# The start of a two-layer encoder: x turned into six banks, scaled parts taken straight from them, and the norm from sums along rows

## What is computed

```python
h = rmsnorm(x, norm_w)                       # x * rsqrt(mean(x*x) + 1e-6) * norm_w
proj = jnp.einsum('bsd,de->bse', h, w_in)    # 1024 -> 9 sections of 1024
qa, ka, va, ga, qh, ffw, fbw, ih, gh = split_cols(proj, EVEN_SIZES)
oa = differential_attention(qa, ka, va, ...) * silu(ga)      # 8 heads
ob = hgrn2_bidirectional(qh, ffw, fbw, ih, ...) * silu(gh)   # 8 heads
x = x + jnp.einsum('bse,ed->bsd', concatenate([oa, ob]), w_out)
```

## Time and profile before

| | before |
|---|---|
| median of 3 executions | 1157.49 us (1157.34 to 1159.63) |
| the profiled execution | 1158.41 us, of it 1156.6 us span |
| TensorE matmul busy | 1127.6 us, 97% |
| DVE busy | 977.4 us, 85% |
| ACT busy | 677.1 us, 59% |
| mean granted TensorE clock | 0.997 |

### The profile page before, as it was taken

How to read it: one execution, slowest core, us unless ns; L and a number is a source line. 1 busy time by engine, 2 the same in 40 slices (tenths; PEclk the granted TensorE clock), 3 DMA queues, 4 the chain that set the end, 5 groups by cost and what they waited for, 6 DMA issues and landing times. The chain is left out here.

```text
span 1156.6 us, 18631 instructions
## 1 busy us (share of the span) xinstructions
PE 1127.6 (97%) x5750; PEld 913.4 (79%) x5750; DVE 977.4 (85%) x1927; ACT 677.1 (59%) x1324; POOL 0.2 (0%) x4
## 2 busy tenths in 40 slices
PE   6999999999999999999999999999999999999996
PEld 5877778778778778778778877887888888888875
DVE  6879889889889889789789898888888888888886
ACT  6474564564564564564654674366666666666654
POOL 0000000000000000000000000000000000000000
PEclk9999999999999999999999999999999999999999
DMA  7613422522422423323324220554232324323112
GB/s 211 158 56 92 138 64 56 145 65 58 130 73 61 121 73 75 107 73 86 96 73 98 85 73 19 124 137 122 80 91 54 91 66 120 101 59 91 55 38 73
DMA packets 131817, 103.60 MB, mean 90 GB/s; under 512 B 5440, under 2 KB 116416, under 8 KB 131776
## 3 DMA queue, kind: packets, MB, share of 16 engines
q1 hardware_dynamic: 131776, 103.07, 32.7%
HBM read 77.88 MB, written 2.10 MB: 69 GB/s over the span
## 5 line engine op out<-in xcount | busy, mean ns | idle before, releaser
L74 PE MATMUL bank_proj<-hH,w_hi 128*128 128x512 f32 x856 | 343.1, 401 | 1.3 <-issue 1.2
L76 PE MATMUL bank_proj<-hH,w_lo 128*128 128x512 f32 x856 | 334.5, 391 | 0.0
L75 PE MATMUL bank_proj<-hL,w_hi 128*128 128x512 f32 x856 | 334.3, 391 | 0.0
L76 PEld LDWEIGHTS bank_proj<-hH,w_lo 128*128 128x128 f32 x856 | 160.8, 188 | 35.2
L74 PEld LDWEIGHTS bank_proj<-hH,w_hi 128*128 128x128 f32 x856 | 161.5, 189 | 32.8 <-issue 1.9
L75 PEld LDWEIGHTS bank_proj<-hL,w_hi 128*128 128x128 f32 x856 | 161.4, 189 | 30.9 <-issue 0.5
L1943 ACT ACTIVATE probs<-bank_odd_score,small 128x256 f32<-128x256 f32 (+1 forms) x128 | 66.3, 525 | 73.9 <-DVE small L2181 73.9
L1220 DVE TENSOR_TENSOR w_lo<-w_raw,w_hi 128x1024 fp32r<-128x1024 f32 x74 | 89.4, 1217 | 9.3 <-ACT w_hi L710 9.3
L710 ACT ACTIVATE w_hi<-w_raw 128x1024 fp32r<-128x1024 f32 x74 | 78.0, 1055 | 28.9 <-DMA w_raw<-in_w_in_even 28.4
L1950 ACT ACTIVATE probsT<-bank_odd_turn 128x256 fp32r<-128x256 f32 (+1 forms) x128 | 49.0, 434 | 61.8 <-PE bank_odd_turn L1677 61.7
L775 ACT ACTIVATE probs<-bank_score,small 128x512 f32<-128x512 f32 x64 | 43.4, 684 | 60.0 <-DVE small L1058 53.2
(11 more groups left out here) (412 smaller groups left out, 2219.0 us busy)
## 6 DMA issues: line engine op xcount, KB each, us to landing
w_raw<-in_w_in_even SPq DMA_DIRECT2D x72, 512.0 KB, 4.9
w_raw<-in_w_in_odd SPq DMA_DIRECT2D x36, 512.0 KB, 4.4
qs<-parts SPq DMA_DIRECT2D x96, 128.0 KB, 2.3
ks<-parts SPq DMA_DIRECT2D x40, 256.0 KB, 4.4
o_raw<-in_w_out_even SPq DMA_DIRECT2D x15, 512.0 KB, 6.2
o_raw<-in_w_out_odd SPq DMA_DIRECT2D x14, 512.0 KB, 6.7
out<-w_raw SPq DMA_DIRECT2D x8, 256.0 KB, 2.1
mixT<-in_x SPq DMA_DIRECT2D x2, 512.0 KB, 5.4
```

Of the source, the lines that this page charges most:

```text
L74: pe.matmul(out, hi, moving_hi, start=start, stop=False)
L75: pe.matmul(out, hi, moving_lo, start=False, stop=False)
L76: return pe.matmul(out, lo, moving_hi, start=False, stop=stop)
```

## The change

SP issues the first weight (-2) between the two halves of x. TensorE turns the eight tiles into six banks (S[0], S[1], T, O, W, PB[2], and S[0], S[1] again), so only tiles 6 and 7 wait: 6 for the first low part and the copy of tile 0, 7 for the copy of tile 1. ACT and DVE form hH and hL straight out of the banks. The copies to xT come later: tile 0 on ACT, all others on DVE, six of them behind the low part of the second weight. On ACT the first weight's high part comes behind the first tile; on DVE its low part too.

The norm's squares are taken from x by rows: four ACT squares of 128 x 1024 with a sum along the row (their own output goes to scratch), into four columns x_squares. One DVE copy spreads each column over 128, and four transposes on TensorE, behind six eighths of projection -1, put the sums of all rows in every partition of T. The root on ACT stands ahead of the high part of weight 1 and not behind it.

On DVE rope scaling comes ahead of the low part of weight 1; the lambda products and the low part of weight 2 come between the first rotation and the values. On TensorE the turning of the values stands behind five eighths of projection 1 and not behind two.

```diff
--- before.py
+++ after.py
@@ -124,12 +124,14 @@
         self.high, self.low = map(sem, ("high", "low"))
         self.xT, self.w, self.hH, self.hL = xT, w, hH, hL
 
-    def split_high(self, act, k):
-        act.activation(self.hH[:, k], self.xT[:, k], ACT.Copy, scale=self.w[:, k:k + 1]).then_inc(self.high.sem, 1)
-
-    def split_low(self, dve, k):
+    def split_high(self, act, k, of=None):
+        of = self.xT[:, k] if of is None else of
+        act.activation(self.hH[:, k], of, ACT.Copy, scale=self.w[:, k:k + 1]).then_inc(self.high.sem, 1)
+
+    def split_low(self, dve, k, of=None):
+        of = self.xT[:, k] if of is None else of
         dve.wait_ge(self.high.sem, self.high.at(0, k + 1))
-        dve.scalar_tensor_tensor(out=self.hL[:, k], in0=self.xT[:, k], scalar=self.w[:, k:k + 1],
+        dve.scalar_tensor_tensor(out=self.hL[:, k], in0=of, scalar=self.w[:, k:k + 1],
                                  in1=self.hH[:, k].bitcast(F32), op0=ALU.mult,
                                  op1=ALU.subtract).then_inc(self.low.sem, 1)
 
@@ -206,6 +208,7 @@
         row_sum, weight = small[:, 16:24], small[:, 24:32]
         lam_t, lam_e = small[:, 32:33], small[:, 34:36]
         total = small[:, 40:48].rearrange("p (d c) -> p d c", d=2)
+        x_squares = small[:, 48:48 + NC]
         att = attT[:, 0:NC * SEQ].rearrange("p (s t) -> p s t", s=NC)
         att_diag = attT[:, :].rearrange("p (c w) -> p c w", w=SEQ + P)[:, :, 0:P]
         key_sum = attT[:, NC * SEQ:2560]
@@ -220,6 +223,9 @@
         O, W = Bank(nc, ctx, "out", 6, -4), Bank(nc, ctx, "wide", 4, -3)
 
         T = Bank(nc, ctx, "turn", 8, 0)
+
+        XB = [S[0], S[1], T, O, W, PB[2], S[0], S[1]]
+        KEPT = (1, 2, 5, 3, 4, 6, 7)
 
         x_landed = [sem(f"x_landed{i}", unit=DMA) for i in range(2)]
         landed = sem("constants_landed", unit=DMA)
@@ -319,10 +325,11 @@
         def _(sp):
             sp.dma_start(eye[:], eye_d).then_inc(x_landed[0].sem, DMA)
             sp.dma_start(wn[:, 0], norm).then_inc(norm_landed.sem, DMA)
-            for i in range(2):
+            def load_x(i):
                 for a in range(2):
                     part = x[2 * a * P:2 * (a + 1) * P, i * SEQ:(i + 1) * SEQ].rearrange("(t p) d -> p t d", p=P)
                     sp.dma_start(x_tiles[a][:, :, i * SEQ:(i + 1) * SEQ], part).then_inc(x_landed[i].sem, DMA)
+
             def load(h, n):
 
                 if w_low.due(h, n - 3):
@@ -377,7 +384,9 @@
                         sp.dma_start(ks[HD * twice:HD * twice + HD, c, :, :].bitcast(F32),
                                      parts[HD * c:HD * c + HD, :, :].bitcast(F32)).then_inc(k_moved.sem, DMA)
 
+            load_x(0)
             load(0, -2)
+            load_x(1)
             load(0, -1)
             sp.dma_start(rope[:], rope_d).then_inc(rope_landed.sem, DMA)
             load(0, 0)
@@ -428,10 +437,12 @@
             for k in range(KT):
                 if k % 4 == 0:
                     pe.wait_ge(x_landed[k // 4].sem, x_landed[k // 4].at(0, 2 if k else 3))
-                if k >= 2:
-                    pe.wait_ge(x_kept[k % 2].sem, x_kept[k % 2].at(0, k // 2))
+                if k == 6:
+                    pe.wait_ge(raw.low.sem, raw.low.at(0, 1))
+                if k >= 6:
+                    pe.wait_ge(x_kept[k % 2].sem, x_kept[k % 2].at(0, 1))
                 for t in range(NC):
-                    mm = pe.transpose(S[k % 2][:, t * P:(t + 1) * P], x_tiles[t // 2][:, t % 2, k * P:(k + 1) * P],
+                    mm = pe.transpose(XB[k][:, t * P:(t + 1) * P], x_tiles[t // 2][:, t % 2, k * P:(k + 1) * P],
                                       eye[:])
                 mm.then_inc(x_turned.sem, 1)
             pe.wait_ge(ready.sem, ready.at(0, 5))
@@ -577,14 +588,19 @@
                 values(h, 1, vh, att)
 
             proj(0, -2)
-            proj(0, -1, 0, 5)
-            rms.sum(pe, T)
-            proj(0, -1, 5)
+            proj(0, -1, 0, 6)
+            pe.wait_ge(rms.added.sem, rms.added.at(0, 1))
+            pe.wait_ge(x_kept[1].sem, x_kept[1].at(0, 2))
+            for t in range(NC):
+                mm = pe.transpose(T[:, t * P:(t + 1) * P], x_rstd[:, t * P:(t + 1) * P], eye[:])
+            mm.then_inc(rms.summed.sem, 1)
+            proj(0, -1, 6)
+            pe.wait_ge(x_kept[1].sem, x_kept[1].at(0, 3))
             proj(0, 0)
-            proj(0, 1, 0, 2)
+            proj(0, 1, 0, 5)
             pe.wait_ge(PB[2].free.sem, PB[2].free.at(0, 0))
             turn(0, 1, vt)
-            proj(0, 1, 2)
+            proj(0, 1, 5)
 
             def iteration(h, first, last):
 
@@ -692,13 +708,14 @@
         @block.scalar
         def _(act):
             act.preload_act_table_set(EXP_LOG)
-            def keep_x(k):
+            def keep_first_x():
+                act.wait_ge(x_turned.sem, x_turned.at(0, 1))
+                act.wait_ge(raw.low.sem, raw.low.at(0, 1))
+                act.activation(xT[:, 0], XB[0][:], ACT.Copy).then_inc(x_kept[0].sem, 1)
+
+            def high_x(k):
                 act.wait_ge(x_turned.sem, x_turned.at(0, k + 1))
-                act.activation(xT[:, k], S[0][:], ACT.Copy).then_inc(x_kept[0].sem, 1)
-
-            def high_x(k):
-                act.wait_ge(x_kept[k % 2].sem, x_kept[k % 2].at(0, k // 2 + 1))
-                raw.split_high(act, k)
+                raw.split_high(act, k, XB[k][:])
 
             def high(h, n):
 
@@ -849,25 +866,21 @@
                         place.then_inc(bank.free.sem, 1)
 
             act.wait_ge(norm_landed.sem, norm_landed.at(0, 1))
-            keep_x(0)
             high_x(0)
+            high(0, -2)
             high_x(1)
-            keep_x(2)
-            high_x(2)
-            high_x(3)
-            keep_x(4)
-            high(0, -2)
-            high_x(4)
-            high_x(5)
-            keep_x(6)
-            high_x(6)
-            high_x(7)
+            keep_first_x()
+            for k in range(2, KT):
+                high_x(k)
             high(0, -1)
-            for k in range(KT):
-                rms.square(act, k)
+            for t, into in enumerate((decay, soft, turned, probs)):
+                for i in range(2):
+                    act.wait_ge(x_landed[i].sem, x_landed[i].at(0, 2 if i else 3))
+                act.activation(into[:, :, :].rearrange("p a t -> p (a t)"), x_tiles[t // 2][:, t % 2, :], ACT.Square,
+                               accum_out=x_squares[:, t:t + 1]).then_inc(rms.squared.sem, 1)
             high(0, 0)
+            rms.root(act, T)
             high(0, 1)
-            rms.root(act, T)
             act.wait_ge(lam_steps.sem, lam_steps.at(0, 2))
             act.activation(lam_e, lam_e, ACT.Exp).then_inc(lam_steps.sem, 1)
             high(0, 2)
@@ -993,7 +1006,7 @@
 
             def keep_x(k):
                 dve.wait_ge(x_turned.sem, x_turned.at(0, k + 1))
-                dve.tensor_copy(xT[:, k], S[1][:]).then_inc(x_kept[1].sem, 1)
+                dve.tensor_copy(xT[:, k], XB[k][:]).then_inc(x_kept[1].sem, 1)
 
             def scale(h, n, into):
 
@@ -1243,29 +1256,27 @@
                                     chunked(bank[:])).then_inc(bank.free.sem, 1)
 
             dve.wait_ge(norm_landed.sem, norm_landed.at(0, 1))
-            keep_x(1)
-            raw.split_low(dve, 0)
-            raw.split_low(dve, 1)
-            keep_x(3)
-            raw.split_low(dve, 2)
-            keep_x(5)
-            raw.split_low(dve, 3)
+            low_x = lambda k: raw.split_low(dve, k, XB[k][:])
+            low_x(0)
             low(0, -2)
-            raw.split_low(dve, 4)
-            keep_x(7)
-            for k in range(5, KT):
-                raw.split_low(dve, k)
+            low_x(1)
+            keep_x(KEPT[0])
+            for k in range(2, KT):
+                low_x(k)
             low(0, -1)
-            for k in range(1, KT):
-                rms.add(dve, k)
+            for k in KEPT[1:6]:
+                keep_x(k)
+            dve.wait_ge(rms.squared.sem, rms.squared.at(0, NC))
+            dve.tensor_copy(chunked(x_rstd[:]), x_squares.unsqueeze(2).broadcast_to([P, NC, P])).then_inc(rms.added.sem, 1)
+            keep_x(KEPT[6])
             low(0, 0)
+            scale_rope()
             low(0, 1)
+            rotate(-1, 7)
             first_lambda()
-            scale_rope()
-            rotate(-1, 7)
+            low(0, 2)
             scale_vt(0, 0, 0)
             rotate(-1, 8)
-            low(0, 2)
             last_lambda()
             scale(0, 1, keys[:, 0])
 
```

## The result

| | before | after |
|---|---|---|
| median of 12 executions each | 1157.88 us | 1159.76 us |
| lowest to highest | 1156.38 to 1159.63 | 1158.74 to 1162.06 |
| the profiled execution | 1158.41, span 1156.6 | 1159.89, span 1157.6 |

The ratio after to before is 1.002, with a 95% interval of 1.0013 to 1.0027: the change costs 1.9 us. That is the direction of the forecast and less than half of its size (4.65 over its own base, 4.2 over this one). Of the 1.9 us, 0.4 lie outside the span, which runs from the first to the last instruction: time less span is 1.72 to 1.90 in every execution of before whose span is on record, and 2.11 to 2.29 in the twelve of after. No profile shows what this is.

What follows compares the result with a forecast made beforehand. TensorE, busy 97%, was taken as the bound, with two chains meeting at the scores. 2.95 later there plus 1.7 for the clock made 4.65: 1163.1 for the profiled execution, 1162.1 forecast, range 1157.0 to 1164.5.

Steps and rivals of the forecast that it cites:

- x and the first weight: Load queue at the start: x's second half lands at 12.2 to 12.3, the first weight at 9.1.
- The turning of x: TensorE's first transposes: waits for x till 12.3, projection starts at 15.8 instead of 16.12, full clock rate at 16.7.
- the rival with the full rate early: TensorE at full rate when x's second half lands: projection at 14.6, total 1158.8 or 1160.5; chance 0.20.
- Scaled parts out of banks: DVE's eight splits reading banks instead of SBUF: 751 against 743 ns each, so no cost.
- The edits ahead of the root bring 0.35: TensorE's chain up to the norm's root: root at 28.0 instead of 28.34, all earlier edits together gaining 0.35 us.
- The new order behind the root, + 3.3: DVE between root and second rotation: added work less removed waits 3.46, taken as 3.3 us after overlap.
- Sum at the scores, 49.2: Start of the first scores: 46.27 - 0.35 + 3.3 = 49.2, or 2.95 us later than before.
- The clock behind that wait, + 1.7: After TensorE's wait ahead of the scores the granted clock falls, costing 1.7 us (ends 0 and 1.7).
- the first rival: The clock stays up at the scores: same chain, 2.95 later, 1160.4 us; chance 0.18.
- the forecast's own case: Scores 2.95 us later plus a clock fall of 1.7: 1161.0 to 1163.5 us; chance 0.36.
- The faster rival: At the 105.70 wait, DVE's own chain comes earlier and the clock does not fall: - 2.9, 1154.6 us; chance 0.12.

Runs made afterwards that it cites:

- after_again: The changed kernel once more, an unaltered copy: 1160.93 us, ratio 1.0024 to before.
- norm_alone: The kernel before with only the new norm (four row squares, one copy, four transposes): 1156.46 us, ratio 0.9987 to before.
- tail_alone: The kernel before with only the new order of work behind the norm's root, old beginning and old norm kept: 1162.12 us, ratio 1.0037 to before.
- lambda_early: The changed kernel with DVE's two lambda products moved ahead of rope scaling, into the wait for the root: 1159.32 us, ratio 1.0015 to before.
- old_tail: The changed kernel with the order of work behind the norm's root put back as before: 1156.61 us, ratio 0.999 to before.

## Why the prediction was right, and where its size was not

- **x and the first weight.** Right: x's second half was issued at 3.78 and landed 8.4 later, at 12.18 (forecast 12.2 to 12.3), and TensorE had a wait there, 0.92.
- **The turning of x.** The middle value, 15.8 with the lower rate to 16.7, is what three of four executions show (15.25 to 15.85, and the products of 512 columns are down to 0.42 or less from 16.68 to 17.19 on); the profiled one took the course of the rival with the full rate early (13.95, there 14.6), and by the times so, it seems, did ten of 22. Both were forecast, and which one an execution takes is not in the program. The Trainium skill, TensorE: Matmul & The Clock Gate (Part 1: The HAM clock gate), says the same of runs of one program, and these four agree: 46.96 to 49.37.
- **Scaled parts out of banks.** Right. DVE's low part lasts 742 to 746 ns out of any bank in after (up to 749 in after_again), 743 out of SBUF before (746 in norm_alone). The 62 cycles more that the Trainium skill, VectorE: DVE Perf Modes (The TRN2 errata), gives an instruction from PSUM do not show.
- **The edits ahead of the root bring 0.35.** Rope scaling is at 27.65, 27.83 and 28.14 in three executions against 28.49 before, so 0.84, 0.66 and 0.35, and 2.81 in the one with the early full rate. norm_alone, at 27.32 with x 0.4 later, adds that the norm is the part that gains.
- **The new order behind the root, + 3.3.** Right in kind and size: from rope's scaling to the scores 17.78 before, 21.28 in after, 21.11 in after_again, 20.91 in tail_alone: + 3.1 to 3.5. The wait between lambda and weight 2 is 1.22 (forecast 1.3), the wait for the values 1.32 (1.6), the wait at the scores 3.03 (2.6). lambda_early, built to take 1.8 of its terms out, brought the scores 1.86 forward.
- **Sum at the scores, 49.2.** 48.76 to 49.37 in three of four executions.
- **The clock behind that wait, + 1.7: this is the term that failed.** The step said that since 2.44 idle at 105.70 brought the clock down, a longer wait would. In none of four executions of the changed kernel did it, after up to 3.03 idle. In tail_alone and lambda_early, with 2.65 and 2.67 idle, it did, for 1.4 and 1.5. The length of the wait does not order them. The price was about right, the rule not, and I had given it 1.7 where it should have been a case beside the other. Without it the forecast is 1160.4, that is the first rival, against the measured 1159.76 and 1160.93. That 1160.4 lies so near is in part luck: the forecast has one course where the kernel has two (scores 0.69 later in one profile, 2.49 to 3.10 in three), and it has no term for the 0.4 outside the span. The median of the first series lies in its stated range and below that of the forecast's own case, 1161.0 to 1163.5.
- **The faster rival** needed DVE's chain up to 105.70 to be DVE's own. The wait there moved by 0.70 with a shift of 0.69 at the scores, and by 108.19 - 105.70 = 2.49 with a shift of 48.76 - 46.27 = 2.49. It fell.

Open: why the wait at the scores brings the clock down in two kernels and not in the four executions of the third. The two that fell have no or only a short wait (none in lambda_early, 0.66 in tail_alone) ahead of the values' transposes, after has 1.32 there; no run varied that alone. Open too is how often an execution of before finds the full rate early. In tail_alone, which has before's beginning, it was there at 11.50 (a pair in 0.41), and the projection still started at 15.81, only 0.3 earlier. And open is whether the missing fall behind 104.86 and 105.04 belongs to norm_alone and old_tail or to their two profiled executions.

## What to carry to other kernels

An engine's gain has to be followed to the next point at which two chains meet; here TensorE came up to 2.8 us earlier to the norm, and the scores were waiting for keys that DVE and two sets of DMAs bring. Before work is put on such a chain, see whether that engine idles ahead of it: DVE waited 2.5 us for the root with the lambda products ready to be done. The low part of weight 1 could have gone there too if its high part had stayed ahead of the root on ACT, which itself waited 2.84 for the sums. Putting the old order back as a whole was worth 3.2 us (old_tail against after; 4.3 against after_again). And an engine that works in program order can hold back work that is ready: ACT stood idle for 6.16 us until 32.69, waiting for DVE's lambda products before its exponential, while weight 2, whose high part stands next in its list, had landed at 28.5. DVE then waited 1.22 for that high part.

## What the runs showed of the hardware that was not expected

- Of two waits of like length one brings TensorE's clock down to 1.2 GHz and the other does not: 2.42 to 2.44 idle at the levels did in ten of the twelve profiles, and did not in old_tail (1.00 in every stretch from 100 to 113) and norm_alone. So too at the scores: 2.65 idle did, 3.03 did not.
- The record of the granted clock says 1.00 from the first instruction, while the first transposes last 0.63 a pair and later 0.38. The first rise can be read off the durations only. (Granted clock from 7 to 20: 1.00 in all twelve profiles.)
- The same program reaches the full rate at about 11 us in one execution (0.56 for the pair at 10.74, 0.44 at 12.22) and behind 16 in three. The first scores are 1.8 to 2.4 us apart between them; the landing of x differs by 0.6 among the same four and is a part of that spread.
- The moves of the keys, 256 KB four times from partition to partition, take 7.0 us to the start of the scores in before, 7.3 in after and 7.65 in old_tail, though nothing in their issue differs (3.16, 3.10 and 3.15 for four).
- Executions of before, tail_alone and norm_alone last 1.72 to 1.91 us longer than their span, those of every kernel with the whole new beginning 2.11 to 2.30. It holds for every execution whose span is on record, and no trace shows what lies there.
